# A two-model kernel on one core: the first input stage works on the stream without its norm

## What is computed

```python
h = rms_norm(x, norm_mix_g[l])            # x / sqrt(mean(x^2) + eps) * g
proj = h @ w_in[l]
cb, cc, cin, q, k, v, f_logit, g_logit = jnp.split(proj, split_idx, axis=-1)
u = causal_dwconv(cc * cin, conv_mix_w[l])
y_conv = (cb * u) @ w_out_conv[l]
log_f = jax.nn.log_sigmoid((f_logit + b_f[l]).astype(jnp.float32))
o = forgetting_attention(q..., k..., v..., log_f)
y_attn = o @ w_out_attn[l]
gates = jax.nn.sigmoid(g_logit + b_gate[l])
x = x + (g_conv * y_conv + g_attn * y_attn) @ w_o[l]
```

## Time and profile before

| what | value |
|---|---|
| median of 3 runs | 2269.43 us (2269.11 to 2273.12) |
| the profiled execution | 2269.96 us, of which its span is 2268.1 us |
| around the span | 1.86 us |
| PE busy | 2231.1 us, 98% of the span |
| POOL, DVE, ACT busy | 1156.1, 1212.7, 835.8 us |
| mean granted clock of TensorE | 0.996 of full speed |

### The profile page before, as it was taken

The page is one execution under the profiler, slowest core; times in us unless marked ns, Lnnn a source line. Parts: engine busy times, 40 slices in busy tenths (PEclk is TensorE's granted clock), DMA queues, the critical chain, the costliest instruction groups (busy, mean ns, idle before and its releaser), DMA issues.

```text
span 2268.1 us, 51407 instructions
## 1 busy us (share of the span) xinstructions
PE 2231.1 (98%) x21811; PEld 1801.4 (79%) x21811; DVE 1212.7 (53%) x2314; ACT 835.8 (37%) x1719; POOL 1156.1 (51%) x803
## 2 busy tenths in 40 slices
PE   8999999999999999999999999999999999999998
PEld 7788888788888677777777777777889788888886
DVE  4353357877830945555555566566540475555521
ACT  4122212333310445555555555555421344434310
POOL 4555567788766253444444444444636343443454
PEclk9999999999999999999999999999999999999999
DMA  3323323333332222222222222222513321221222
GB/s 116 84 77 82 84 87 91 92 97 98 94 112 84 66 71 68 69 76 72 76 81 80 69 69 78 69 69 97 172 49 120 103 75 52 63 56 50 67 106 93
DMA packets 262109, 188.04 MB, mean 83 GB/s; under 512 B 18284, under 2 KB 242410, under 8 KB 261498
## 3 DMA queue, kind: packets, MB, share of 16 engines
q1 hardware_dynamic: 261881, 184.76, 27.2%
HBM read 162.69 MB, written 22.04 MB: 81 GB/s over the span
## 4 chain that ended last, share of the span: by engine, by line
PE 92%; DVE 3%; POOL 3%; ACT 1%; issue 0%; SPq 0%; DMA 0%; POOLq 0%; DVEq 0%; ACTq 0%
PE ps L1359 19%; PE ps L162 16%; PE ps L163 15%; PE ps L164 15%; PE ps L1545 3%; PE ps L1561 3%; PE ps L1587 2%; PE ps L2495 2%; PE ps L1534 2%; PE ps L1372 1%; PE ps L1501 1%; PE ps L227 1%; PE ps L1473 1%; PE ps L1490 1%; PE ps L1523 1%; PE ps L1459 1%
## 5 line engine op out<-in xcount | busy, mean ns | idle before, releaser
L153 POOL TENSOR_TENSOR w_lo<-raw,w_hi 128x1024 fp32r<-128x1024 f32 (+1 forms) x177 | 450.1, 2543 | 14.8
L150 POOL TENSOR_SCALAR w_hi<-raw 128x1024 fp32r<-128x1024 f32 (+1 forms) x177 | 196.0, 1107 | 478.1 <-PE ps L164 462.1
L162 PE MATMUL ps<-h_hi,w_hi 128*128 128x512 f32 x616 | 243.6, 395 | 1.8 <-DVE h_lo L1068 1.7
L164 PE MATMUL ps<-h_hi,w_lo 128*128 128x512 f32 x616 | 240.8, 391 | 0.0
L163 PE MATMUL ps<-h_lo,w_hi 128*128 128x512 f32 x616 | 240.4, 390 | 0.0
L1359 PE MATMUL ps<-mixed_k,raw 128*64 128x264 f32 x1024 | 149.3, 387 | 0.0
L1359 PE MATMUL ps<-mixed_r,raw 128*64 128x264 f32 x1024 | 144.0, 387 | 0.0
L1359 PE MATMUL ps<-mixed_g,raw 128*64 128x264 f32 x1024 | 137.9, 386 | 0.0
L162 PEld LDWEIGHTS ps<-h_hi,w_hi 128*128 128x128 f32 x616 | 116.3, 189 | 26.1 <-DVE h_lo L1068 2.7
L164 PEld LDWEIGHTS ps<-h_hi,w_lo 128*128 128x128 f32 x616 | 116.0, 188 | 24.9
L163 PEld LDWEIGHTS ps<-h_lo,w_hi 128*128 128x128 f32 x616 | 116.1, 189 | 23.1
(11 more groups left out here) (464 smaller groups left out, 5931.5 us busy)
## 6 DMA issues: line engine op xcount, KB each, us to landing
raw<-in_rwkv_w_in_dram SPq DMA_DIRECT2D x64, 512.0 KB, 4.2
raw<-in_w_up_dram SPq DMA_DIRECT2D x44, 512.0 KB, 3.8
raw<-in_w_in_dram SPq DMA_DIRECT2D x41, 512.0 KB, 3.9
raw<-in_w_down_dram SPq DMA_DIRECT2D x22, 512.0 KB, 3.6
raw<-in_mla_w_in_dram SPq DMA_DIRECT2D x22, 512.0 KB, 4.0
sb_kept<-xT SPq DMA_DIRECT2D x16, 528.0 KB, 2.8
xT<-sb_kept SPq DMA_DIRECT2D x16, 528.0 KB, 4.5
raw<-in_rwkv_w_out_dram SPq DMA_DIRECT2D x16, 512.0 KB, 3.9
```

Of the source, the lines that this page charges most:

```text
L150: nc.gpsimd.tensor_scalar(w_hi[s][:, 0:width], raw[s][:, 0:width], 1.0, 0.0, ALU.mult, ALU.add).then_inc(split_hi, 1)
L153: nc.gpsimd.tensor_tensor(w_lo[s][:, 0:width], raw[s][:, 0:width], w_hi[s][:, 0:width].bitcast(F32), ALU.subtract).then_inc(split_ready, 1)
L162: nc.tensor.matmul(dst, w[0], x[0], start=start, stop=False)
L164: return nc.tensor.matmul(dst, w[1], x[0], start=False, stop=stop)
```

## The change

- **No norm in the turn.** PE turns seven of the eight raw x tiles at once, each into a bank of its own (`raw_bank`), and the eighth inside the first strip, ahead of its product k = 5. `h_hi` and `h_lo` are taken from these banks (times the gain g, without r), and the residual's copy `xT` from the same banks. The 32 matmuls against `x_diag` go, as do the turns between the strips.
- **The root comes later.** Four matmuls of a matrix of ones with `x_diag` spread r over all partitions; DVE copies it to `r_in` and makes `r_in2` = r^2.
- **Every strip's result is multiplied.** DVE multiplies f, q, k and the gates by `r_in` and cc by `r_in2`; the conv's taps get one more product with `r_in`. ACT takes q, k, f and the gates from these copies in SBUF. The v rows get r as the scale of ACT's copy, which is now four instructions.
- **Order.** SP loads only parameter group 1 (with the gain) ahead of the first two weight strips, and the other two groups and `b_f` behind them. POOL splits strip 0 ahead of the root's power. PE runs strips 0, r, 1, 2, 3 and then turns parameter groups 0 and 2. ACT squares the meta rows first.
- Sizes, splits and everything behind the first attention are as before.

```diff
+                    if k == KD - 3:
+                        pe.wait_ge(x_copied, 2)
+                        raw_turn(pe, KD - 1)
                     pe.wait_ge(h_lo_ev, k + 1)
                 mm = product(ps[:, s, :], block_of(s, k), h_x(k), k == 0, k == KD - 1)
...
-                pe.wait_ge(x_copied, KD)
+                pe.wait_ge(x_step, R_IN + 1)
...
+        def raw_bank(j):
+            return 1 + j % 7
+
         def raw_turn(pe, j):
-            pe.wait_ge(x_copied, 4 if j < 6 else j - 1)
             for t in range(QB):
-                mm = nc.tensor.transpose(ps[:, 6 + j % 2, t * P:t * P + P], x_rows[:, t, j * P:j * P + P], ident[:])
+                mm = nc.tensor.transpose(ps[:, raw_bank(j), t * P:t * P + P], x_rows[:, t, j * P:j * P + P], ident[:])
             mm.then_inc(x_turned, 1)
...
-                for j in range(4):
-                    mm = nc.tensor.transpose(ps[:, 4 + j, t * P:t * P + P], x_rows[:, t, j * P:j * P + P], ident[:])
+                for j in range(KD - 1):
+                    mm = nc.tensor.transpose(ps[:, raw_bank(j), t * P:t * P + P], x_rows[:, t, j * P:j * P + P], ident[:])
                     if t == QB - 1:
                         mm.then_inc(x_turned, 1)
+            pe.wait_ge(s_tab, FIRST_PARAMS)
+            params_turn(pe, 1, 0)
+            pe.wait_ge(p_turned, P_FIRST)
+            in_strip(pe, 0)
+            pe.wait_ge(x_step, X_SCALE + QB + 1)
+            pe.wait_ge(cst, PADDED)
+            for t in range(QB):
+                mm = nc.tensor.matmul(ps[:, raw_bank(1), t * P:t * P + P], ones[:], x_diag[:, t, :], start=True, stop=True)
+            mm.then_inc(x_step, 1)
+            pe.wait_ge(x_copied, 3)
+            for u in range(1, 4):
+                in_strip(pe, u)
+            pe.wait_ge(s_meta, 16)
             pe.wait_ge(s_in, N_IN)
-            for g in range(3):
-                n = ROWS_USED[g]
-                nc.tensor.transpose(ps[:, 0, g * P:g * P + n], p_rows[0:n, g, :], ident[0:n, 0:n]).then_inc(p_turned, 1)
+            pe.wait_ge(x_copied, KD)
+            for g in (0, 2):
+                params_turn(pe, g, 6)
             for j in range(KD):
-                if j >= 3:
-                    pe.wait_ge(h_lo_ev, j - 2)
-                for t in range(QB):
-                    if j == 0:
...
-            pe.wait_ge(p_turned, P_COPIED)
-            in_strip(pe, 0)
-            in_strip(pe, 1)
-            raw_turn(pe, 4)
-            raw_turn(pe, 5)
-            in_strip(pe, 2)
-            raw_turn(pe, 6)
...
-            act.wait_ge(unit_done, u + 1)
             if kind == "gate":
-                nc.scalar.activation(gates[:, j, :], src, ACT.Tanh, scale=0.5, bias=prm("b_gate", j)).then_inc(free[u % 2], 1)
...
+                act.wait_ge(free[u % 2], USES[u] + 1)
+                nc.scalar.activation(gates[:, j, :], gates[:, j, :], ACT.Tanh, scale=0.5, bias=prm("b_gate", j))
             elif kind == "q":
+                act.wait_ge(scaled, 2 * j + 2)
                 for e in range(2):
-                    nc.scalar.activation(q_main[own1[e], e, :], ps[own1[e], u % 2, :], ACT.Copy, scale=HD1 ** -0.5).then_inc(qk_act, 1)
-                    nc.scalar.activation(q_bias[own1[e], e, :], ps[own1[e], u % 2, :], ACT.Copy, scale=HD1 ** -0.5).then_inc(qk_act, 1)
+                    nc.scalar.activation(q_main[own1[e], e, :], strip[own1[e], 0, :], ACT.Copy, scale=HD1 ** -0.5).then_inc(qk_act, 1)
...
         def front_act(act):
+            act.wait_ge(s_meta, 16)
+            act.wait_ge(cst, ZEROED)
+            nc.scalar.activation(x_sq[0:N_META, :], meta_rows[:], ACT.Square, accum_out=x_ss[0:N_META, 0, QB:QB + 1]).then_inc(x_step, 1)
             for t in range(QB):
                 act.wait_ge(x_land[t], 16)
-                if t:
-                    act.wait_ge(x_step, t)
+                act.wait_ge(x_step, t + 1)
...
+            act.wait_ge(p_turned, P_FIRST)
+
+            def high(j):
+                act.wait_ge(x_turned, j + 1)
+                nc.scalar.activation(h_hi[:, j, :], ps[:, raw_bank(j), :], ACT.Copy, scale=prm("g_mix", j)).then_inc(h_hi_ev, 1)
+
+            def raw_out(j):
+                act.wait_ge(h_lo_ev, j + 1)
+                nc.scalar.activation(xT[:, j, 0:T1], ps[:, raw_bank(j), :], ACT.Copy).then_inc(x_copied, 1)
+            for j in range(3):
+                high(j)
+            raw_out(0)
+            high(3)
+            raw_out(1)
+            for j in range(4, KD):
+                high(j)
             nc.scalar.activation(ident_b[:], ident[:], ACT.Copy)
             nc.scalar.activation(causal_b[:], causal[:], ACT.Copy)
-            act.wait_ge(p_turned, P_COPIED)
-            for j in range(KD):
-                act.wait_ge(h_mm, j + 1)
-                nc.scalar.activation(h_hi[:, j, :], ps[:, 1 + j % 3, :], ACT.Copy, scale=prm("g_mix", j)).then_inc(h_hi_ev, 1)
...
+            act.wait_ge(s_in, N_IN)
+            act.wait_ge(scaled, 1)
+            nc.scalar.activation(fl[FROWS, 0, :], strip[FROWS, 0, :], ACT.Identity, bias=b_f[FROWS, 0:1]).then_inc(free[0], 1)
...
-            nc.scalar.activation(v_rows[:], ps[:, 2:6, :], ACT.Copy).then_inc(v_out, 1)
+            act.wait_ge(x_step, X_ROOT)
+            for t in range(QB):
+                mv = nc.scalar.activation(v_rows[:, t, :], ps[:, 2 + t, :], ACT.Copy, scale=x_ss[:, 2, t:t + 1])
+            mv.then_inc(v_out, 1)
...
+            dve.wait_ge(unit_done, u + 1)
+            if kind == "gate":
+                nc.vector.tensor_tensor(gates[:, j, :], src, r_in[:], ALU.mult).then_inc(free[s], 1)
+            elif kind == "conv" and part == 0:
+                nc.vector.tensor_tensor(cc[:], src, r_in2[:], ALU.mult).then_inc(free[s], 1)
...
-                dve.wait_ge(c_step, 4 * j + 3)
-                nc.vector.tensor_tensor(cz[:], cu[:, 0, :], src, ALU.mult).then_inc(free[s], 1)
+                dve.wait_ge(c_step, 5 * j + 4)
+                nc.vector.tensor_tensor(cz[:], cu[:, 1, :], src, ALU.mult).then_inc(free[s], 1)
...
             elif kind == "q":
+                nc.vector.tensor_tensor(strip[:, 0, :], src, r_in[:], ALU.mult).then_inc(scaled, 1)
                 for e in range(2):
                     dve.wait_ge(qk_act, 8 * j + 2 + 2 * e)
-                    mv = nc.vector.scalar_tensor_tensor(out=q_main[own1[1 - e], e, :], in0=ps[own1[e], s, :], scalar=HD1 ** -0.5,
+                    mv = nc.vector.scalar_tensor_tensor(out=q_main[own1[1 - e], e, :], in0=strip[own1[e], 0, :], scalar=HD1 ** -0.5,
...
-                dve.wait_ge(unit_done, u + 1)
+                nc.vector.tensor_tensor(strip[:, 1, :], src, r_in[:], ALU.mult).then_inc(scaled, 1)
...
-                    mv = nc.vector.tensor_tensor(k_bias[own1[e], e, :], ps[own1[e], s, :], k_main[own1[e], e, :].bitcast(F32),
+                    mv = nc.vector.tensor_tensor(k_bias[own1[e], e, :], strip[own1[e], 1, :], k_main[own1[e], e, :].bitcast(F32),
...
+            dve.wait_ge(c_step, 5 * j + 3)
+            nc.vector.tensor_tensor(cu[:, 1, :], cu[:, 0, :], r_in[:], ALU.mult).then_inc(c_step, 1)
...
+            dve.wait_ge(p_turned, P_FIRST - 1)
+            params_out(1, 0)
+            dve.wait_ge(p_turned, P_FIRST)
+            for j in range(4):
+                low_part(j)
             dve.wait_ge(x_step, X_ROOT)
             for t in range(QB + 1):
                 nc.vector.tensor_scalar(x_diag[:, t, :], ident[:], x_ss[:, 2, t:t + 1], None, ALU.mult).then_inc(x_step, 1)
-            dve.wait_ge(p_turned, P_COPIED)
-            nc.vector.tensor_scalar(prm("b_gate", 0, 16), prm("b_gate", 0, 16), 0.5, None, ALU.mult).then_inc(p_turned, 1)
...
-            for j in range(4):
-                dve.wait_ge(x_turned, j + 1)
-                nc.vector.tensor_copy(xT[:, j, 0:T1], ps[:, 4 + j, :]).then_inc(x_copied, 1)
+            for j in range(4, KD):
+                low_part(j)
+            dve.wait_ge(x_copied, 2)
+            for j in (KD - 1, *range(2, KD - 1)):
+                nc.vector.tensor_copy(xT[:, j, 0:T1], ps[:, raw_bank(j), :]).then_inc(x_copied, 1)
+            dve.wait_ge(x_step, R_MM)
+            nc.vector.tensor_copy(r_in[:], ps[:, raw_bank(1), :]).then_inc(x_step, 1)
+            dve.wait_ge(x_step, R_IN)
+            nc.vector.tensor_tensor(r_in2[:], ps[:, raw_bank(1), :], r_in[:], ALU.mult).then_inc(x_step, 1)
+            dve.wait_ge(x_step, R_IN + 1)
+            dve.wait_ge(unit_done, 1)
+            nc.vector.tensor_tensor(strip[FROWS, 0, :], ps[FROWS, 0, :], r_in[FROWS, :], ALU.mult).then_inc(scaled, 1)
...
+                params_out(g, 6)
+            dve.wait_ge(p_turned, P_COPIED)
...
+            split_unit(pool, 0, 0, first=True)
             pool.wait_ge(x_step, X_MEAN)
             nc.gpsimd.tensor_tensor(x_ss[:, 2, :], x_ss[:, 1, :], eps_col[:, 3:4].broadcast_to([P, QB + 1]), ALU.pow).then_inc(x_step, 1)
-            for u in range(2):
-                split_unit(pool, u, u % 2, first=True)
+            split_unit(pool, 1, 1, first=True)
...
```

(12 more changed lines are left out.)

## The result

The changed kernel takes **2284.22 us** (median of 4 runs, 2280.42 to 2286.45), the kernel before 2269.27 us on the same chip (2268.78 to 2273.12). The ratio is **1.0055**, with a 95% interval of 1.004 to 1.007: slower, by some 12 to 15 us. The forecast was 2275.4 with a range up to 2279.5, so the sign was right and the size less than half of it. The profiled execution takes 2282.98 us, its span is 2281.1 us, 13.0 us longer than before.

What follows compares the result with a forecast made beforehand. PE, busy for 98% of the span, was taken as the bound. Strip 3's delay 1.3, low clock 2.7, parameter turns 0.25 and attention 1.7 sum to 5.95, so 2269.43 + 6.0 = 2275.4 us; range 2270.0 to 2279.5.

Steps and rivals of the forecast that it cites:

- The first weight: Head: load issued at about 5.6, POOL's split from 10.7, weight ready at 14.2, strip 0 9.9 us sooner.
- Rival 5: Head: strip 0 held to about 17 by the weight's landing, strip 3 at 46.5; 2278, chance 0.05.
- The products of strip 0 at the low clock: Strip 0: products start 0.42 us apart, five tiles take to 20.0 to 20.5, clock rises after some 5 us.
- `x_diag`: DVE's products in the head: no time added; the eighth tile's low part was put at 22.2.
- From there to strip 3: DVE and ACT from 22.2 until q's bank is free: strip 3 begins at 43.9, 1.3 us later; bounds 41.5 to 45.
- the hold-up of the casts: DVE's forget gate chain ahead of strip 3: POOL's split of strip 4 holds up the casts, running to 38.4.
- The clock behind the wait: Strip 3 starts at the low clock after PE's 9 us idle: loss 2.7 us, bounds 2.3 to 3.1.
- the parameter turns: Two parameter turns on PE behind strip 3: 0.25 us, bounds 0.2 to 0.5.
- Attention: 32 more DVE products: k's bank 0.45 us three times, some 0.4 at L499; sum 1.7, bounds 0 to 4.
- Rival 1: Ahead of strip 3: q's bank released by 34.7, head start kept, 7.9 us won; 2263.5, chance 0.06.
- Rivals 2 and 3: Second: casts run between POOL's instructions, strip 3 at 41.5, 2272.3, chance 0.17. Third: attention hides all, 2273.7, chance 0.17.
- Rival 4: Attention: DVE becomes late, its 22 us more cost 4 or more, strip 3 at 45; 2279.5, chance 0.12.

Runs made afterwards that it cites:

- after: The changed kernel itself, compared with the kernel before: 2284.22 us, ratio 1.0055.
- E3: Changed kernel, POOL begins strip 1's split only when the five x_diag products are done: 2283.39 us, ratio 1.0058 to the kernel before.
- E1: Changed kernel, q's bank given back by the product with r, for pair 0 ahead of the forget gate's chain: 2270.03 us, ratio 1.0000.
- E2: Changed kernel, POOL begins strip 4's split only when the forget gate's chain is done: 2279.17 us, ratio 1.0044 to the kernel before.
- E4: Changed kernel with 34 spare matmuls on PE between strips 2 and 3, read by nobody: 2280.07 us, ratio 1.0047 to the kernel before.
- E6: Changed kernel with E1, the waits of E3 and E5, and k's two decay products ahead of k's product with r: 2262.66 us, ratio 0.9965.
- E5: Changed kernel, POOL begins strip 12's split only when DVE has normalised pair 0, block 1: 2278.02 us, ratio 1.0035 to the kernel before.
- E7: Kernel before with one unused DVE product of two SBUF inputs added in each conv strip's taps: 2273.86 us, ratio 1.0017.
- E8: E6 with the second weight strip's load issued seven small loads later: 2263.01 us, ratio 0.9968 to the kernel before.
- E9: Kernel before, POOL's split of strip 12 waits until the normalisation has written all its blocks: 2270.22 us, ratio 0.9997.
- E10: E6 with 15 spare 128x128 products on PE ahead of strip 0, read by nobody: 2260.87 us, ratio 0.9964 to the kernel before.

## Why the prediction was off, step by step

- **The first weight: too early.** I had its split begin at 10.7 and end at 14.2 (13.3 to 15); it began at 12.27 (issued at 5.55, as worked out), and strip 0 started at 15.85, outside these bounds. From issue to POOL's start it took 6.7 us, where the row that I priced it by had 4.2; I had added 0.9 for the x tiles that are still landing. Error: 1.6 us in this execution, 0.8 in the best of the eight with this order of loads (14.96). Rival 5 had this place, but at 17.
- **The products of strip 0 at the low clock: right in pace.** They follow each other every 0.43 us (forecast 0.42). How long this lasts differs: up to 18.9 in after, 3 us behind the first product, and up to 21.0 in E3, 6 us behind it; the forecast had 5 to 6. The matmuls of L615, from which I took the low clock, stand at a granted clock of 1.00 in the records (last section), so this came out right in part by luck.
- **`x_diag`: the term that I had taken at its old price.** Its five instructions lasted 1.06 us before, and the prediction gave them nothing. The change puts POOL's split of strip 1 beside them. 3.98 us, low part 4 late, a wait of 1.5 us for PE. Without the meeting only 0.4 us came back, because the products stayed slow for longer there (E3). I had asked for POOL's splits at strips 3 and 4, but not for each instruction of DVE that comes to stand beside another one of POOL. The eighth low part ends at 24.67 instead of 22.2, 2.5 us late: 1.6 from the weight and 0.9 from behind it, which `x_diag` explains in part.
- **From there to strip 3: right to half a microsecond.** Copies, ACT's steps, two hold-ups beside POOL (2.77 and 2.44 us), q's 3.8 us: 22.3 us where the sum had 21.7. The mechanism, q's bank held until the forget gate's chain is through, is confirmed by E1; the hold-up of the casts by E2. The start of strip 3 was forecast at 43.9 and came at 46.96; the bound was 45. That is 3.1 of the 7 us that are missing.
- **The clock behind the wait: right.** 2.7 forecast; 2.9 by E4, 3.06 with the parameter turns (forecast 2.95 for both).
- **Attention: the mis-sized term, and the step that failed most.** Forecast +1.7, of which 0.4 for the place where L499 waits; measured +6.2. The three waits for k's bank were forecast at 0.45 each and shift what follows by 0.4 each, 0.5 us of it in all as PE's own wait (E6 removes them by the order alone). The other place cost 5.0 us. I saw that the product with r delays POOL's split and that the wait of L499 would grow. What I did not do is follow the two engines to the *next* meeting: with 0.27 us of room at the meeting behind the one of the earlier trace rows (DVE at 90.69, POOL at 90.96), a shift of 0.3 us turns the order round, and then it is not 0.3 us that are lost but POOL's whole split. E5 and E7 show it from both sides. And I priced the wait without the clock behind it, which doubled it in the profiled execution: PE waits 2.4 us more than before, and the stretch is 5.0 us longer. The bound "0 to 4" was too small by that.
- **The rivals.** Rival 1 (head start kept) is what E1 and E6 make true. Its condition alone, the early release, gave 2270.03 us (E1), where its working had 2263.5: it took over the attention at +1.7. Only with the meetings taken away as well came 2262.66; that this lies by 2263.5 is in part luck, since the working counted 1.7 for the attention that E6 no longer pays and a head start of 7.9 us that was not reached (meta products 6.8 ahead). Rivals 2 and 3 fell: the casts met POOL, and the attention hid nothing of what counted. Rival 4 has the time nearest to the result, and half its reason: DVE was late in the attention, but not as a whole; one instruction was.
- **The sum in total.** Missing are 3.1 at strip 3, 0.1 behind it and 4.5 in the attention, 7.7 in all; 0.6 come back behind 256 us, which leaves 7.1 (13.0 less the 5.95 of the sum). These 0.6 are a balance of drops of the clock that fall in different places in the two executions (before has one from 408 to 412 us that after lacks) and say nothing of the change. The medians lie 15.0 us apart, the ratio says 12.5; the runs of after spread over 6 us.

The Trainium skill, "SBUF — State Buffer", section "Who interferes with whom", states an exclusive lock on a port pair, held for a whole instruction, with the order of issue deciding. The runs agree in both directions: the pair of `a_p` takes 0.62 us with POOL still (E5), 1.45 when it comes 0.27 us first (before; only its second instruction meets POOL), and 3.59 when it comes 0.03 us second (after); on the other side POOL's `w_hi` takes 1.32 us when it comes 0.27 us behind a DVE product, where it takes 1.04 alone. The page says of a DVE instruction in a two-port mode and GpSimd that "the other fully blocks", and for DVE the price here is indeed that of what is left of the other engine's instruction, as the ends of the two instructions of L984 show. For POOL beside the product with r it is less: 0.28 us, where the product had 0.42 us left.

## What to carry to other kernels

When a step is added to an engine that shares something with another, list each meeting of the two engines with the room that it has, and price a meeting with less room than the shift at the other's whole instruction, plus what TensorE's low clock behind the wait costs (here 1.3 us in E7 and 2.6 in after, behind waits of 3.2). When a change brings an earlier start, look first for the bank or buffer that is given back last: here the release moved to another instruction (E1) was worth 12.5 us, more than the 8.3 us by which strip 0 starts sooner. And before reading a difference of a microsecond or two off two profiled executions, look whether both start strip 0 at the same time and have the same drops of the clock. Give a buffer back at the first instruction that has copied it out, not at the last of the chain.

## What the runs showed of the hardware that I had not expected

- **Two short waits bring the clock down like one long one, and for how long differs.** In after the waits of 1.26 and 1.93 us, with two small turns between them, were followed by a granted clock of 0.50 to 0.60 from 102 to 108 us; so it was in E3 and E4. In E1, E2 and E7, with the same waits, it was low for under 4 us (in E7 from about 93.5 to 96.9). From the end of strip 8 to the first eight products with v it takes 31.4 to 31.5 us in the first three and 30.0 to 30.4 in the other three. Waits of 0.8 us (before) and 0.4 (E5, E6) there were followed by no drop.
- **The clock can fall with PE busy.** Behind the meta products (small matmuls, 24 records of L636 and L640, 16x16) the granted clock fell for about 4 us with no wait of PE in seven of the twelve profiled executions: E1 (45 to 49 us), E2 (56 to 60), E4 (54 to 58), E5 (55 to 60), E8 (44 to 49), E9 (51 to 55) and E10 (42 to 46). It did not in before, after, E3, E6 and E7. From the meta products to the end of strip 8 it takes 31.5 us in the seven and 29.9 in the five, so the drop costs 1.6 us. I have no run that tells why in some and not in others. Other drops (near 400, 820, 1670 and 1770 us) stand behind a wait or idle time of PE, as at 1767 us in the earlier trace rows, and those near 400 and 1670 are not in each execution. This may be a part of the 6 to 8 us over which ten or more runs of one kernel spread, which was not shown; it does show why one profiled execution can't settle a difference of 2 us.
- **The granted clock of the records is not the whole story.** In the kernel before it reads 1.00 in all windows from 8 to 26 us, while the weight loads of L615 last 333 ns up to about 19.4 us and 192 behind. The prediction took this for a low clock, which no record shows. In E6 the products of strip 0 are as slow and the records do say 0.50. For the kernel before this stays open.
- **Five instructions of 128x128 lasted as long as POOL's split**, 3.98 us for 1.07: the small size of an instruction is no protection, it is the neighbour's size that sets the price.
